# One inference step of a hybrid encoder layer on one core: the output projection and the second norm moved into the mixers' stage

## The reference, cut to what matters

```python
u = rmsnorm(h, lp['g_mix'])
z = u @ lp['w_in']                       # 3072 columns, six parts
oA, S_new = hgrn2_mixer(...)             # head group A: 4 heads of 128 channels
oB, h_new, buf_new = rglru_mixer(...)    # head group B: 512 channels
h = h + jnp.concatenate([oA, oB], axis=-1) @ lp['w_out']
h = h + peer(rmsnorm(h, lp['g_ffn']), lp['w_peer_q'], lp['peer_keys'], lp['peer_u'], lp['peer_v'])
h = h + (p_l @ lp['w_ple']) * jax.nn.sigmoid(rmsnorm(h, lp['g_ple']) @ lp['w_ple_gate'])
return rmsnorm(h, g_final), S_new, h_new, buf_new
```

## Time and profile before

| | |
|---|---|
| median of 3 runs | 3327.52 us (3323.61 to 3328.42) |
| the profiled execution's own time | 3322.15 us |
| its span, first to last instruction | 3320.4 us |
| busy share of the span: PE, DVE, ACT, POOL | 94%, 80%, 33%, 32% |
| mean granted TensorE clock, as a share of 2.4 GHz | 0.977 |

### The profile page before, as it was taken

How to read it: one execution, slowest core, us unless ns; L and a number is a source line. 1 busy time by engine, 2 the same in 40 slices (tenths; PEclk the granted TensorE clock), 3 DMA queues, 4 the chain that set the end, 5 groups by cost and what they waited for, 6 DMA issues and landing times. The chain is left out here.

```text
span 3320.4 us, 50638 instructions
## 1 busy us (share of the span) xinstructions
PE 3131.3 (94%) x17340; PEld 2840.7 (86%) x17340; DVE 2659.9 (80%) x4821; ACT 1095.9 (33%) x1441; POOL 1065.6 (32%) x834
## 2 busy tenths in 40 slices
PE   7999977999689999999999999799999999999988
PEld 6999956899689999999999999688888888888877
DVE  5344434688889999999999987499999999999954
ACT  5545522111212322255555532222222222222242
POOL 1111100111055454544444455233343343333300
PEclk9999988999899999999999999899999999999999
DMA  4211141110499999999999999799999999999911
GB/s 116 61 51 52 40 179 21 36 43 22 132 323 277 289 283 297 294 307 326 325 325 318 329 350 349 261 351 356 352 373 345 366 343 353 354 357 353 332 45 57
DMA packets 402059, 808.94 MB, mean 244 GB/s; under 512 B 36128, under 2 KB 256176, under 8 KB 394544
## 3 DMA queue, kind: packets, MB, share of 16 engines
q0 software_dynamic: 110592, 402.70, 36.2%
q1 hardware_dynamic: 269488, 304.44, 29.3%
q10 hardware_dynamic: 21888, 100.67, 7.7%
HBM read 692.02 MB, written 115.68 MB: 243 GB/s over the span
## 5 line engine op out<-in xcount | busy, mean ns | idle before, releaser
L1413 POOL DMA_INDIRECT h<-in_peer_u,ga_rows x384 | 560.7, 1460 | 641.5 <-DVE ea_acc L1864 462.2
L255 PE MATMUL ea_pa<-rest_hi,ea_uhi 128*128 128x384 f32 x2048 | 699.9, 342 | 54.9 <-DVE ea_ulo L1729 52.0
L257 PE MATMUL ea_pa<-rest_hi,ea_ulo 128*128 128x384 f32 x2048 | 687.9, 336 | 0.0
L256 PE MATMUL ea_pa<-rest_lo,ea_uhi 128*128 128x384 f32 x2048 | 687.8, 336 | 0.0
L1413 POOL DMA_INDIRECT eo_ring<-in_peer_v,ga_rows x384 | 406.5, 1059 | 686.3 <-DVE h L2163 629.1
L2163 DVE SCALAR_TENSOR_TENSOR h<-eo_ring,eo_share,h 128x1024 f32<-128x1024 f32 x384 | 490.6, 1278 | 0.0
L1864 DVE CUSTOM_DVE_ANT_0 h<-h,plain 128x1024 f32<-128x1024 f32 x384 | 454.7, 1217 | 36.4 <-DMA h<-in_peer_u,ga_rows 36.2
L255 PEld LDWEIGHTS ea_pa<-rest_hi,ea_uhi 128*128 128x128 f32 x2048 | 386.6, 189 | 64.4 <-DVE ea_ulo L1729 27.3
L256 PEld LDWEIGHTS ea_pa<-rest_lo,ea_uhi 128*128 128x128 f32 x2048 | 387.3, 189 | 0.0
L257 PEld LDWEIGHTS ea_pa<-rest_hi,ea_ulo 128*128 128x128 f32 x2048 | 386.7, 189 | 0.0
L2099 ACT ACTIVATE eo_phi<-eo_prod 128x512 fp32r<-128x512 f32 x192 | 121.6, 633 | 773.6 <-DVE eo_prod L2137 727.9
(11 more groups left out here) (334 smaller groups left out, 5777.9 us busy)
## 6 DMA issues: line engine op xcount, KB each, us to landing
ea_raw<-in_peer_u SPq DMA_DIRECT2D x512, 128.0 KB, 7.1
region<-in_peer_v SPq DMA_DIRECT2D x128, 512.0 KB, 11.7
act_scratch<-ea_stage ACTq DMA_DIRECT2D x128, 384.0 KB, 6.4
w_scratch<-region ACTq DMA_DIRECT2D x24, 2048.0 KB, 9.6
region<-w_scratch SPq DMA_DIRECT2D x16, 1536.0 KB, 13.2
region<-act_scratch SPq DMA_DIRECT2D x16, 1536.0 KB, 17.4
eo_wt<-w_scratch SPq DMA_DIRECT2D x16, 1536.0 KB, 14.3
eo_at<-act_scratch SPq DMA_DIRECT2D x16, 1536.0 KB, 18.0
```

The costliest lines, as they stand in the source:

```text
L255: nc.tensor.matmul(out, w[0], x[0], start=first, stop=False)
L256: nc.tensor.matmul(out, w[0], x[1], start=False, stop=False)
L257: return nc.tensor.matmul(out, w[1], x[0], start=False, stop=last)
L1413: nc.gpsimd.indirect_dma_start(out=dst, out_offset=None, in_=table, in_offset=bass.IndirectOffsetOnAxis(ap=self.rows[:, m % GT, m // GT:m ...
```

## The change

The three blocks become one: `output_projection` and `norm_transpose` are gone, and their work stands at the end of each engine's list in `project_and_mix`. All on-chip buffers get fixed addresses (`Space`), so that the projection's buffers can lie over the split input `xhi`, `xlo` once the last group is summed. Heads 0 to 2 of both groups still go through `cat_scratch`; the last head's two results stay on chip (`cat`). Rows of `w_out` are taken in the order 0, 1, 2, 4, 5, 6, 3, 7 (`ORDER`), the first six of which need only heads 0 to 2 (`EARLY` = 6). Rows 0 and 1 of that order use the input weights' buffers, rows 2 to 7 are loaded once the last group is summed. All eight low parts are made on POOL. PE sums the first six rows of tile 0 behind `outputs` of the last head and those of tile 1 behind `outputs_back`, then the last two rows of both, then tiles 2 to 8 whole; each summed tile is normed while the next is summed, its transposes standing behind the sixth row of the next tile.

```diff
 SP, after the loop over the heads:
+                e.wait_ge(summed, GROUPS)
+                e.wait_ge(cat_b_out, (HA - 1) * 16)
+                e.wait_ge(cat_a_out, (HA - 1) * 16)
+                late_weights(2)
+                mixed(0)
+                late_weights(3)
+                late_weights(4)
+                mixed(1)
+                for j in range(5, KC):
+                    late_weights(j)
                 store_states(HA - 1)
                 store_rg(HA - 1)
-                store_hgrn(HA - 1)
+                e.wait_ge(all_used, HA)
+                for t in range(NT):
+                    load_tokens(P, e, t)
+                e.wait_ge(olo_done, 2)
+                e.dma_start(gain[:], a["g_ffn"][0].rearrange("(a n) -> a n", a=1).broadcast_to([128, D])
+                            ).then_inc(gain2_in, 16)
+                for t in range(2, NT):
+                    e.wait_ge(o_summed, t - 1)
+                    mixed(t)
+                keys.load(e, 0, 0)
 POOL, after the input weights:
+                for j in range(KC):
...
+                    e.wait_ge(ohi_done, j + 1)
+                    nc.gpsimd.tensor_tensor(lo, rest, hi.bitcast(F32), ALU.subtract).then_inc(olo_done, 1)
 ACT, after the groups:
+                c_hi(0)
+                out_hi(2)
+                out_hi(3)
+                c_hi(1)
                 output_squares(HA - 1)
+                out_hi(4)
                 output_root(HA - 1)
+                for j in range(5, KC):
+                    out_hi(j)
+                last_hi(0)
+                last_hi(1)
+                e.wait_ge(st_out, HA * 2 * 16)
+                for t in range(NT):
+                    for before in {0: (), 1: (), 2: (0, 1)}.get(t, (t - 1,)):
+                        x2_hi(before)
+                    squares2(t)
+                    if t + 2 < NT:
+                        e.wait_ge(o_summed, t + 1)
+                        c_hi(t + 2)
+                        last_hi(t + 2)
+                    root2_of(t)
+                x2_hi(NT - 1)
 DVE, last head and after:
                     state_chain(i)
+                    if i == HA - 1:
+                        c_lo(0)
+                        c_lo(1)
                     side_output(i)
                     output(i)
+                last_lo(0)
+                last_lo(1)
+                for t in range(NT):
+                    for before in {0: (), 1: (), 2: (0, 1)}.get(t, (t - 1,)):
+                        x2_lo(before)
+                    add(t)
+                    mean2_of(t)
+                    if t + 2 < NT:
+                        c_lo(t + 2)
+                        last_lo(t + 2)
+                    norm2(t)
+                keep_plain(0)
+                keep_plain(1)
+                x2_lo(NT - 1)
+                keep_plain(2)
 PE, after the groups:
                 outputs(HA - 1)
+                e.wait_ge(z_ready, GROUPS)
+                for j in range(EARLY):
+                    out_product(0, j)
                 outputs_back(HA - 1)
+                for j in range(EARLY):
+                    out_product(1, j)
+                for t in range(2):
+                    for j in range(EARLY, KC):
+                        out_product(t, j)
+                for t in range(2, NT):
+                    e.wait_ge(added, t - 1)
+                    for j in range(KC):
+                        out_product(t, j)
+                        if t == 2 and j == 1:
+                            turn2(0)
+                        if j == EARLY - 1:
+                            turn2(t - 1)
+                turn2(NT - 1)
...
-def output_projection(P, cat_dram):
...
-def norm_transpose(P, name, gain, xhi, xlo, blocks=False, beside=None, plain=None):
...
```

520 lines of the change are left out of this document (217 added, 303 removed).

## The result

The changed kernel takes 3291.89 us in the median of 4 runs (3290.22 to 3301.45), the kernel before 3327.2 in runs beside it: a ratio of 0.9902, with a 95% interval of 0.9881 to 0.9922. A second comparison, with six runs of the changed kernel, gave 0.9910 (0.9893 to 0.9927). The prediction was 3301.0 and faster. The profiled execution took 3290.24 us, its span 3288.5.

A forecast was written before the change was run, and what follows sets the result against it. Before the route stage, idle time, PE's products and a norm chain over nine tiles took 156.4 us; 8.0 + 20.1 + 85.8 + 16.0 = 129.9 saves 26.5, giving 3295.7, or 3301.0 as a median, range 3288 to 3314.

The forecast's parts named there:

- last head's end later than 430.26: Last head's final multiplication: ends at 438.3, 8.0 us later, delayed by copies, POOL's low parts and DVE meeting POOL.
- from there to tile 2: Last head's end to tile 2's start: 20.1 us, its pieces queued behind nine token tiles and the gain.
- last sum to first route product: Behind the last tile: remaining norm, block's end and split of the first route weights, 16.0 us against 40.7 before.
- the lower bound: Last head's end with POOL and DVE free of each other: sixth low part near 431.4, end at 435.4.
- the meeting of DVE and POOL: At the last head: POOL subtractions hold DVE operations; one meeting gives 437.5, two 439.1, middle 438.3.
- the other addresses change no list: Moved buffers in the whole program: an edit costed at nothing.
- The fourth rival: Later stages run 1.0% slower, 27 us, through other addresses and first loads: 3328, no change; chance 0.04.
- The early start is worth little by itself: Tiles 0 and 1 on PE ahead of the last head's end: without it 3303, inside the range.
- No stall, with 0.3 us to spare: Norm inside tiles 2 to 8: no PE wait while pieces land under 3.8 us after the sum.
- The first rival: Last head and loads cost nothing, tile 2 follows near 448 without clock loss: 38.9 us less, 3288.6; chance 0.10.
- The third: Rival: pieces land late, at 11.7 us, 7.9 wait per tile, 21 us slower than before: 3348; chance 0.04.
- the upper bound: Last head's end at 441, if the small DVE operations behind are held by POOL too.

The follow-up runs named there:

- e8: The kernel before with only the changed kernel's on-chip addresses for the buffers from the norm on: 3316.26 us, 0.9978.
- e2: The changed kernel with PE turning the last head first, then doing tiles 0 and 1 whole: 3294.37 us, 0.9912.
- e4: The changed kernel with PE turning the last head after five rows of tile 0 instead of six: 3290.03 us, 0.9895.
- e5: The changed kernel with the pieces of tile t + 2 issued when tile t's squares are done, not its sum: 3307.47 us, 0.9947.
- e6: The changed kernel with tiles 2 and 3's pieces and gain ahead of tokens, last head turned after five rows, splits ahead of squares and mean: 3284.62 us, 0.9878.
- e7: The changed kernel with the DRAM buffer for the channels 8 rows wide again instead of 6: 3291.78 us, 0.9905.
- e9: e6 plus the route stage's first weights split ahead of the barrier and the third plain copy ahead of the last low part: 3278.46 us, 0.9858.
- e3: The changed kernel with all tiles' transposes, high and low parts behind the last tile's sum, scaling left in place: 3315.17 us, 0.9974.

## Why the prediction was right, and where it was off

It said faster, 3301.0 with 3288 to 3314; it became 3291.9. By its own terms, for the two traces of the changed kernel:

| term | predicted | measured |
|---|---|---|
| last head's end later than 430.26 | 8.0 | 8.1 and 8.8 |
| from there to tile 2 | 20.1 | 18.3 and 19.5 |
| tiles 2 to 8 | 85.8 | 86.9 and 86.9 |
| last sum to first route product | 16.0 | 15.6 and 15.5 |
| sum, against 156.4 | 129.9 | 128.8 and 130.7 |
| behind the route's start | 0 | -4.3 in both, against 2733.7 |

**The chain in front came out as worked out in its sum, and one term of it by luck.** The saving in it, 26.5, was 27.6 in the first pair of traces and 26.4 in the second. The last head's 8.0, however, was made up otherwise than predicted. ACT in the changed kernel:

```profile
424.88 0.84 ACT L569 ACTIVATE op_chi<-op_c_raw 128x768 fp32r<-128x768 f32 x1 [1.30 <-DMA op_c_raw<-cat_scratch]
...
425.63 1.12 ACT L694 ACTIVATE h<-pm_ps 128x1152 f32<-128x1152 f32 x1
```

Tile 1's pieces were there at 424.88, not at 422.5 (SP's first issue was at 414.84, not at 413.5, and the queue took longer), so the squares began at 425.63, not at 423.3, and POOL's sixth low part ended near 434.2 where the lower bound had 431.4. Of these 2.8 us the meeting of DVE and POOL, to which the prediction had given all of its 2.9, made 0.4. (At its own 2.0 a meeting, two of them would give 439.4, not 439.1.) The 20.1 to tile 2 erred the other way: the pieces landed 16.2 us after the first token load, where 18.2 had been worked out.

**The term that failed is the last, "the other addresses change no list" costed at nothing.** The lists are indeed the old ones, but the addresses were worth 7.3 us (e8), about a fifth of the whole gain. That figure is measured on the kernel before; in the two traces of the changed kernel the rest is 4.3 to 7.9 shorter than in the two of the kernel before. The fourth rival looked at this very thing with the wrong sign: it let the later stages only become slower. "I see no row in which an address matters" was a reason to leave the sign open, not to leave the gain out. The median came 9.1 under the 3301.0: 1.1 from the front, 4.3 from behind the route's start, and 3.7 from the base, since the profiled execution of the kernel before lay 5.4 under its median and that of the changed kernel 1.65. This last part says nothing of the change.

**"The early start is worth little by itself": right** (e2, 0.7 us in the medians). Its own price was seen too: it is what PE does while the last head waits for its turn (e4).

**"No stall, with 0.3 us to spare": nearly right.** In the changed kernel one of six sets waited, 0.67 us; with 2.8 us more, each set with pieces loading ahead of it waited some 2 and one 4.29 (e5). The pieces ahead of the set that waited 0.67 landed 4.8 us after their issue, so the limit is nearer to 4.1 than to the 3.8 of the prediction; the price of 13 to 15 us at 6 us of landing stands.

**The first rival** gave 3288.6, near what came (3291.9), but not by its mechanism: the idle time ahead of tile 2 was there, and the clock loss too. What it describes is e6, where the front saved 586.7 - 551.6 = 35.1 of the 38.9 it spoke of. **The third** would have needed landings that no trace showed.

**DVE beside POOL.** The prediction took one or two meetings, and as a sign of them DVE operations of 2 to 3 us. None of the changed kernel's first trace is that long; the second has one of 2.08. This is the first (timeline, DVE and POOL at the last head):

```profile
425.76 1.33 DVE L937 TENSOR_TENSOR op_clo<-op_c_raw,op_chi 128x768 fp32r<-128x768 f32 x1 [4.27 <-ACT op_chi L569]
...
427.01 1.35 DVE L913 TENSOR_TENSOR op_cat<-mx_xc,h 128x1152 f32<-128x1152 f32 x1
...
428.48 1.33 DVE L922 TENSOR_REDUCE mx_rs<-h 128x9 f32<-128x1152 f32 x1
...
429.85 0.75 DVE L923 TENSOR_SCALAR mx_rs<-mx_rs 128x9 f32<-128x9 f32 x1
...
427.77 2.79 POOL L529 TENSOR_TENSOR op_wlo<-op_w_raw,op_whi 128x1024 fp32r<-128x1024 f32 x1 [1.50 <-ACT op_whi L565]
```

The split of tile 1 took 1.33 instead of the 0.96 of the others. The small operation at 429.85 took 0.75 and ended with POOL's subtraction, at 430.60 and 430.56; in e7, with POOL idle beside it, it took 0.17. The sum over rows at 428.48 took its usual 1.33 beside the same subtraction. And this is e7, with the same lists:

```profile
424.50 2.49 DVE L937 TENSOR_TENSOR op_clo<-op_c_raw,op_chi 128x768 fp32r<-128x768 f32 x1 [3.10 <-ACT op_chi L569]
...
426.91 3.54 DVE L913 TENSOR_TENSOR op_cat<-mx_xc,h 128x1152 f32<-128x1152 f32 x1
...
431.94 0.17 DVE L923 TENSOR_SCALAR mx_rs<-mx_rs 128x9 f32<-128x9 f32 x1
...
426.51 2.72 POOL L529 TENSOR_TENSOR op_wlo<-op_w_raw,op_whi 128x1024 fp32r<-128x1024 f32 x1 [0.33 <-ACT op_whi L565]
...
433.38 7.01 POOL L529 TENSOR_TENSOR op_wlo<-op_w_raw,op_whi 128x1024 fp32r<-128x1024 f32 x3 [4.15 <-ACT op_whi L565]
...
435.79 0.58 PE L157 MATMUL pm_ps<-op_whi,op_chi 128*128 128x512 f32 x1 [4.84 <-POOL op_wlo L529]
```

Group B's gate, 1.35 above, took 3.54 as if it began only when POOL's fifth subtraction was done, at 429.23. Everything behind it moved: the root on ACT, the copies behind the root, POOL's sixth subtraction from 431.87 to 433.38, and PE waited 4.84 us. The last head ended at 441.48, half a microsecond beyond the upper bound. In all ten traces with these lists it goes by which of the two begins first. In seven the gate begins no later than POOL's fifth subtraction (427.01 and 427.77 in the changed kernel); there the gate takes 1.34 to 1.35 and POOL 2.79 to 3.56 instead of some 2.4. In e6, e7 and e9 POOL begins 0.10 to 0.40 earlier; there the gate takes 3.52 to 3.54. The start of DVE's split does not decide it: 424.52 in the changed kernel's second trace, 424.50 here.

TensorE's clock moves this term as well. The turning of the last head in the changed kernel, and in e3, which has the same lists up to here:

```profile
435.78 1.14 PE L1128 MATMUL pm_ps<-ident,mx_kdtok 128*128 128x128 f32 x9
```

```profile
435.81 2.12 PE L1125 MATMUL pm_ps<-ident,mx_kdtok 128*128 128x128 f32 x9
```

The granted clock from 436 to 438 was 1.00 (2.4 GHz) in the first and 0.50 (1.2 GHz) in the second, and the head ended 1.0 later, at 439.40. PE had waited 2.00 us ahead of the sixth row in both; what made the clock fall in one and not in the other no row shows. Of the six traces with this order the changed kernel's first is the only one that turned the head at full clock, which the prediction's 1.1 for the transposes takes for granted. So this term has a spread of 3 us between executions that no single trace shows.

The Trainium skill (SBUF — State Buffer, Who interferes with whom) has an instruction with two SBUF inputs exclude a POOL instruction that reads SBUF, and also says that `tensor_scalar` can enter a mode that uses both ports while `tensor_reduce` cannot on this chip; the traces agree with all three (the gate's 3.54 against 1.35; 0.75 against 0.17; 1.33 beside POOL as alone). The prediction had left that mode out and held every operation with one SBUF input to be safe.

## What to carry to other kernels

Ask first which part of a many-part change is on the path: of this one, hiding the second half of the norm behind the next tile's products carried some 23 us, moved buffers 7, the early start nothing that can be measured. When a queue of loads feeds the next step, reordering it moves the wait to whichever load is last; look for loads that can leave the queue altogether, as the gain did in e6. Cost moved addresses from both sides, and measure them alone, by giving the old kernel the new addresses.

## What the runs showed of the hardware that I had not expected

The on-chip address of a buffer changed how soon loads into it land, 13.2 to 10.9 us for 1.5 MB from the same DRAM buffer (before and e8), and the kernel's time by 0.2%; the place of the DRAM buffer did not (e7). That the sooner landing is what shortens the time is not shown. The same lists gave a last head's end anywhere from 438.38 to 441.48 over six traces: through the clock granted to nine transposes (1.14 or 2.12 us), and through meetings of DVE and POOL, which held the split of tile 1 for 0.4 to 1.5 us in all six and the gate for 2.2 in one. And the last pieces, with other loads right behind them in SP's list, landed later than the pieces of the other tiles: 2.41 instead of 1.15 to 1.35 us of waiting, and 6.02 instead of 3.56 to 3.93 in e5. That those other loads are the reason is only argued.
